# A mixed-layer inference step on one core: gate products placed one by one, states written out in two halves, expert weights loaded earlier, and 72 instead of 48 weight chunks on eleven places

## The reference, cut to what matters

```
P  = rmsnorm(x) @ w_in                      # 1024 x 5888, split among heads and two gates
x  = x + (sigmoid(G_a) * (HGRN2(P) @ w_branch_a) + sigmoid(G_b) * (RWKV7(P) @ w_branch_b)) @ w_out
x  = x + moe(rmsnorm(x))                    # 32 experts, top 4 per token
y  = rmsnorm(x)

def expert_block(tok, e):                   # every expert runs
    h = x[tok] @ w_gu[e] + b_gu[e]          # 1024 x 2048
    act = glu * sigmoid(1.702 * glu) * (lin + 1.0)
    return act @ w_down[e] + b_down[e]      # 1024 x 1024
```

## Time and profile before

| | us |
|---|---|
| median of three runs | 1326.92 (1326.70 to 1327.52) |
| the profiled execution, its own time | 1327.32 |
| its span, first to last instruction | 1325.6 |
| PE busy | 1288.1 (97%) |
| DVE, ACT, POOL busy | 373.8, 242.4, 52.6 |

### The profile page before, as it was taken

One profiled execution on the slowest core, in us unless ns is written; L12 is line 12 of the kernel. 1 busy time (PEld: TensorE's weight loads), 2 busy tenths in 40 slices (PEclk: granted clock), 3 DMA queues, 4 the chain that ended last, 5 costly groups with the idle time before them and its releaser, 6 DMA issues.

```text
span 1325.6 us, 18387 instructions
## 1 busy us (share of the span) xinstructions
PE 1288.1 (97%) x7355; PEld 615.1 (46%) x7355; DVE 373.8 (28%) x1019; ACT 242.4 (18%) x532; POOL 52.6 (4%) x127
## 2 busy tenths in 40 slices
PE   8999999999999999999999999999999999999997
PEld 6778768888754333333333333333333333233333
DVE  3234666554327212121121211212112111211112
ACT  3143343222122101111111111111111101111102
POOL 5000200000050000000000000000000000000000
PEclk9999899999999999999999999999999999999999
DMA  7635426110779999999999999999999999999996
GB/s 232 173 97 190 129 64 198 62 37 33 281 290 375 411 430 427 429 429 428 424 412 429 429 429 430 430 430 430 430 429 430 429 429 430 431 428 429 429 429 278
DMA packets 72720, 449.40 MB, mean 339 GB/s; under 512 B 14388, under 2 KB 43110, under 8 KB 47864
## 3 DMA queue, kind: packets, MB, share of 16 engines
q1 hardware_dynamic: 67090, 445.72, 82.2%
q10 hardware_dynamic: 5574, 2.88, 0.8%
HBM read 443.82 MB, written 4.76 MB: 338 GB/s over the span
## 4 chain that ended last, share of the span: by engine, by line
PE 75%; DMA 18%; DVE 4%; ACT 2%; issue 1%; ACTq 0%; SPq 0%; DVEq 0%
PE bank L1254 24%; PE bank L1274 13%; PE bank L553 8%; DMA ring<-in_expert_w_gu_dram 7%; PE bank L1162 5%; DMA arena<-in_expert_w_gu_dram 5%; PE bank L1193 4%; PE bank L657 3%; DMA extra<-in_expert_w_down_dram 3%; PE bank L1064 2%; DMA extra<-in_expert_w_gu_dram 2%; PE bank L1038 2%; PE bank L931 2%; ACT arena L1400 1%; PE bank L1169 1%; PE bank L914 1%
## 5 line engine op out<-in xcount | busy, mean ns | idle before, releaser
L1254 PE MATMUL bank<-arena 128*64 128x512 f32 x960 | 216.6, 594 | 1.0 <-DMA arena<-in_expert_w_gu_dram 1.0
L1400 ACT ACTIVATE arena<-bank 128x512 f32<-128x512 f32 (+6 forms) x232 | 115.5, 516 | 494.3 <-PE bank L1274 195.9
L1254 PE MATMUL bank<-ring,arena 128*64 128x512 f32 x848 | 189.6, 594 | 3.5 <-DMA ring<-in_expert_w_gu_dram 3.5
L1400 ACT ACTIVATE arena<-arena 128x256 f32<-128x256 f32 (+7 forms) x124 | 69.0, 565 | 470.9 <-DVE arena L2339 463.8
L2339 DVE TENSOR_SCALAR arena<-bank 128x256 f32<-128x256 f32 x64 | 27.0, 422 | 379.2 <-PE bank L1254 379.2
L1254 PEld LDWEIGHTS bank<-arena 128*64 128x64 f32 x960 | 67.2, 137 | 134.5 <-issue 116.9
L553 PE MATMUL bank<-arena,ring 128*128 128x288 f32 (+1 forms) x464 | 118.8, 417 | 0.5 <-ACT arena L1400 0.5
L1254 PEld LDWEIGHTS bank<-ring,arena 128*64 128x64 f32 x848 | 59.7, 137 | 115.4 <-issue 100.0
L2388 DVE COPY arena<-bank 64x512 f32<-64x512 f32 x30 | 20.8, 694 | 319.6 <-PE bank L1274 319.6
L553 PEld LDWEIGHTS bank<-arena,ring 128*128 128x128 f32 x464 | 89.0, 193 | 28.5 <-issue 1.9
L1274 PE MATMUL bank<-arena 128*64 128x512 f32 x448 | 100.6, 595 | 0.0
(11 more groups left out here) (371 smaller groups left out, 1130.7 us busy)
## 6 DMA issues: line engine op xcount, KB each, us to landing
arena<-in_expert_w_gu_dram SPq DMA_DIRECT2D x60, 2048.0 KB, 23.5
ring<-in_expert_w_gu_dram SPq DMA_DIRECT2D x53, 2048.0 KB, 20.6
ring<-in_expert_w_down_dram SPq DMA_DIRECT2D x28, 2048.0 KB, 20.5
arena<-in_expert_w_down_dram SPq DMA_DIRECT2D x28, 2048.0 KB, 26.8
extra<-in_expert_w_gu_dram SPq DMA_DIRECT2D x15, 2048.0 KB, 22.5
ring<-in_w_in_dram SPq DMA_DIRECT2D x23, 1024.0 KB, 5.4
extra<-in_expert_w_down_dram SPq DMA_DIRECT2D x7, 2048.0 KB, 31.7
ring<-in_w_out_dram SPq DMA_DIRECT2D x4, 1024.0 KB, 7.0
```

The source lines that it names most:

```text
L1254: ins = mm(bank[q % 2][64 * (q // 2):64 * (q // 2) + 64, :], gu_lhs(c), w[:, q * 512:(q + 1) * 512], start=(c == 0), stop=(c == KT - 1), s ...
L1400: return nc.scalar.activation(out, in_, f, **kw)
```

## The change

- Gate products are no longer placed by tiles in the front but by single products: 3, 3, 2, 5, 1, 1, 1, 8 in the samples' RWKV stage, then 1, 1, 1, 2, 1, 9, 6, 3 and the rest up to 56 in the HGRN2 stage. In the units the four products of site Y move to A5, which then has five; the sum of a unit stays 18.
- The HGRN2 states of the samples go out in two transfers of 1 MB, after `hg_upd` 4 and 8. DVE waits for the first before its masks, ACT for the second before the first squares.
- The last two w_out chunks are loaded when the HGRN2 stage has ended; chunk 3 is issued right behind chunk 2, chunks 0 and 4 before the wait for `merged` 8, chunk 5 behind it.
- 72 chunks instead of 48 use eleven places (`HEAD_QUADS` = 3): three quads are written out, and the eight places come after.
- For the first pair POOL makes `ind`, and PE no longer waits for `gsel_ready` before the first expert's bias; the wait stands before `gt_T`.
- PE runs seven spare products, five before the first transposes and two before the first projection.

```diff
-WS, FULL = 8, 11
+WS, FULL, HEAD_QUADS = 8, 11, 3
-        PEELED = 2 * QUAD * ECH
+        PEELED = HEAD_QUADS * QUAD * ECH
-        btmp = PQ[:, 0:NT]
+        btmp = fm[9][:, 0:NT]
-        FILL = (("Y1", 1), ("A0", 1), ("A1", 1), ("A3", 1), ("A4", 1), ("A5", 1), ("Y", 4), ("k0", 0), ("k1", 0), ("k2", 0), ("k3", 1),
+        FILL = (("Y1", 1), ("A0", 1), ("A1", 1), ("A3", 1), ("A4", 1), ("A5", 5), ("Y", 0), ("k0", 0), ("k1", 0), ("k2", 0), ("k3", 1),
                 ("c0", 2), ("c1", 1), ("c2", 1), ("c3", 3))
...
-            for n in list(range(N_IN + 4)) + [N_IN + 6, N_IN + 7, N_IN + 4, N_IN + 5]:
+            for n in list(range(EARLY)) + [N_IN + 6, N_IN + 7] + list(range(EARLY, N_IN + 6)):
                 if n == N_IN + 6:
-                    sp.wait_ge(S("oa_done"), 9)
+                    sp.wait_ge(S("hg_state"), 8)
+                    sp.wait_ge(S("hg_o_evac"), 3)
                     sp.wait_ge(S("rws_out"), 16 * NB)
                 if n == N_IN + 4:
                     sp.wait_ge(S("rwp_out"), 16)
                     w_load(sp, 0, 2)
+                    w_load(sp, 0, 3)
...
+            w_load(sp, 0, 0)
+            w_load(sp, 0, 4)
             sp.wait_ge(S("merged"), 8)
-            w_load(sp, 0, 0)
             for x in (0, 2, 3):
                 sp.dma_start(braw[NE * x:NE * x + NE, :], expert_b_gu[0]).then_inc(S("braw_loaded"), 16)
-            for s in (3, 5):
-                w_load(sp, 0, s)
-            sp.wait_ge(S("wo_done"), 1)
-            w_load(sp, 0, 4)
+            w_load(sp, 0, 5)
...
+            keep_busy(5, bank[5])
             for t, (o, n) in enumerate(TILES):
                 pe.wait_ge(S("xn_done"), t + 1)
...
+            keep_busy(2, bank[5])
             pe.wait_ge(S("xT_evac"), 5)
...
+            def gate_run(to):
+                while gate_m[0] < to:
...
+            def gate(n):
+                gate_run(gate_m[0] + n)
...
-                gate_tile()
+                gate(3)
                 for G in range(2):
+                    if G:
+                        gate(3)
                     for b in range(NB):
...
-                gate_tile()
+                gate(5)
                 for j in range(3):
+                    if j:
+                        gate(1)
...
                 if t:
-                    gate_tile()
+                    gate(3)
                 pe.wait_ge(S("hg_kT_evac"), i3 + 1)
                 if t:
                     pe.wait_ge(S("hg_upd"), 8)
...
                 if t:
-                    gate_tile()
+                    gate_run(KT * WHOLE)
                 for c in range(4):
...
+                    if t == 0:
+                        gate(1)
                     pe.wait_ge(S("hg_state"), g)
...
                 for g in range(2):
-                    gate_tile()
+                    gate((9, 6)[g])
...
             pe.wait_ge(S("hg_state"), 8)
-            pe.wait_ge(S("rw_in"), 1)
...
-            pe.wait_ge(S("bgu3"), 1)
+            pe.wait_ge(S("bgu3"), 2)
...
                     if c == 6:
-                        if x == 0:
+                        if x == 0 and not first:
                             pe.wait_ge(S("gsel_ready"), i + 1)
...
                     if x == 1:
+                        pe.wait_ge(S("gsel_ready"), i + 1)
                         gt_T()
...
+            def sample_states_out(g):
+                act.wait_ge(S("hg_upd"), 4 * g + 4)
+                b = slice(4 * g, 4 * g + 4)
+                act.dma_start(hgrn_s[0, b].rearrange("b h k v -> k (b h) v"),
+                              s0h.rearrange("p (b h v) -> p b h v", b=NB, h=HA)[:, b].rearrange("p b h v -> p (b h) v"))\
+                   .then_inc(S(f"hgrn_out{g}"), 16)
...
+                    sample_states_out(0)
                     keys_evac(2, 1)
-                    act.wait_ge(S("hg_upd"), 8)
-                    act.dma_start(hgrn_s[0].rearrange("b h k v -> k (b h) v"), s0h.rearrange("p (b h v) -> p (b h) v", b=NB, h=HA))\
-                       .then_inc(S("hgrn_out"), 16)
+                    sample_states_out(1)
...
+                if u == 0:
+                    act.wait_ge(S("hgrn_out1"), 16)
                 square_evac(0)
...
-                    dve.wait_ge(S("hgrn_out"), 16)
+                    dve.wait_ge(S("hgrn_out0"), 16)
...
+            for x in range(2):
+                step(g.tensor_scalar(ind[:, x * SLOTS:(x + 1) * SLOTS], bcast(pmod, [P, SLOTS]), float(x), None, ALU.is_equal), "bgu3")
```

More of the change, by code:

```diff
@@ L312, in pe_place @@
         def pe_place(quad, s):
-            return place((quad if isinstance(quad, int) else 2) * (QUAD * ECH) + s)
+            return place((quad if isinstance(quad, int) else HEAD_QUADS) * (QUAD * ECH) + s)
         def pe_w_wait(quad, s):
@@ L323, in pe_w_wait @@
                 per_quad = QUAD * ECH // WS
-                nc.tensor.wait_ge(w_loaded[place(n)], quad * (16 * per_quad) + 16 * (loads_into(place(n), n + 1) - 2 * per_quad))
+                nc.tensor.wait_ge(w_loaded[place(n)], quad * (16 * per_quad) + 16 * (loads_into(place(n), n + 1) - HEAD_QUADS * per_quad))
         def acc(t):
@@ L475, in expert @@
                 return sp.value_load(bt[0:1, bass.ds(quad * QUAD + j, 1)], min_val=0, max_val=NE - 1)
-            with sp.Fori(3, last) as quad:
+            with sp.Fori(HEAD_QUADS + 1, last) as quad:
                 for j in range(QUAD):
@@ L534, in _, with keep_busy @@
             done(i, "par_T")
+            def keep_busy(n, b=bank[1]):
+                for _ in range(n):
+                    mm(b[:, 0:P], ident, ones, start=True, stop=True)
+            keep_busy(5, bank[5])
             for t, (o, n) in enumerate(TILES):
@@ L628, in _ @@
                 done(i, "smp_pe")
[L630 to L649, removed]
+            gate_m = [0]
+            def gate_run(to):
+                while gate_m[0] < to:
                     g, kt = gate_m[0] // KT, gate_m[0] % KT
@@ L660, in fill @@
                         done(i, "pj_done")
+            def gate(n):
+                gate_run(gate_m[0] + n)
+            def fill(u, site):
+                gate_run(gate_products(u, site))
             vR, At, Rt, Bn, Kn = fm[2], fm[5], fm[6], fm[7], fm[8]
@@ L743, in smp_states @@
                     done(i, "smp_pe")
-                gate_tile()
+                gate(8)
                 for q in range(4):
@@ L751, in _ @@
             smp_scores()
+            gate(2)
             smp_solve()
@@ L1100, in last_logits @@
                 return i
-            def keep_busy(n, b=bank[1]):
-                for _ in range(n):
-                    mm(b[:, 0:P], ident, ones, start=True, stop=True)
             w_out_tile(2, acc(2))
@@ L1364, in pe_last @@
                     done(ins, "wo_done")
-            for quad in range(2):
+            for quad in range(HEAD_QUADS):
                 for p in range(2):
@@ L1370, in _ @@
             last = pe.value_load(nblk[0:1, 1:2], min_val=0, max_val=(BLOCKS - NE) // QUAD) + (NE // QUAD - 1)
-            with pe.Fori(2, last) as quad:
+            with pe.Fori(HEAD_QUADS, last) as quad:
                 for p in range(2):
@@ L2366, in gather_rows @@
                 for x in range(2):
-                    v.tensor_scalar(ind[:, x * SLOTS:(x + 1) * SLOTS], ones[:, 0:SLOTS],
-                                    gselc[:, x * TW + 6:x * TW + 7], None, ALU.mult)
+                    if not (isinstance(i, int) and i == 0):
+                        v.tensor_scalar(ind[:, x * SLOTS:(x + 1) * SLOTS], ones[:, 0:SLOTS],
+                                        gselc[:, x * TW + 6:x * TW + 7], None, ALU.mult)
                     ins = onehot(gsel, x * SLOTS, P, gselc[:, x * TW:x * TW + 3], gselc[:, x * TW + 3:x * TW + 6])
@@ L2524, in _ @@
                 step(g.tensor_tensor(braw[r, :], braw[r, :], bgu3[r, :], ALU.subtract))
-                i = g.tensor_copy(bgu3[r, :], braw[r, :])
-                step(i, "bgu3" if r.start == 96 else "pool_step")
+                step(g.tensor_copy(bgu3[r, :], braw[r, :]))
+            for x in range(2):
+                step(g.tensor_scalar(ind[:, x * SLOTS:(x + 1) * SLOTS], bcast(pmod, [P, SLOTS]), float(x), None, ALU.is_equal), "bgu3")
             pool.wait_ge(S("logits"), 2)
```

12 lines of the change are left out of this document (6 added, 6 removed).

## The result

The changed kernel takes 1320.17 us (median of five runs, 1319.95 to 1320.58) against 1327.52 (1326.70 to 1327.93) of the kernel before on the same chip: a ratio of 0.9944, 95% interval [0.9931, 0.9956], 7.35 us less. The prediction was 1317.4, inside its range of 1313.0 to 1322.0, and 2.8 us too low: 2.15 because the gain was to be 9.5 us and is 7.35, 0.6 because the kernel before takes 1327.52 us here and not the 1326.92 from which the forecast was counted. The profiled execution took 1319.95 us, its span is 1318.2.

The account below looks back on a forecast made before the run. The prediction took the weight stream from chunk 6's issue to bound the kernel: -4.2 and -2.2 us until chunk 6, then -1.4 and -1.7 for holes, -9.5 in all, giving 1317.4 us, range 1313.0 to 1322.0.

Parts of the forecast that it names:

- What bounds the kernel: Whole kernel: the weight stream sets the end, counting from chunk 6's issue, which the front's PE work decides.
- The check of the sum: Weight stream: chunk 6's issue at 399.8, 185 chunks, two holes and slow start give 1306 to 1309, against 1306.9.
- Gate products before R: Front, before the units: single products keep the clock at 1.00 and fill idle PE time; -4.2 us (bounds -1.0 and -5.9).
- the clock falls all the same: Rival, front near 156 us: the clock still halves despite the split, so 2.4 us is missing, 1319.8; chance 0.20.
- Spare products: Front, before first transposes and projection: seven products' cost stands against an earlier clock rise; 0 (bounds +0.5 and -0.8).
- States in halves: Front, before unit 0's masks: both 1 MB transfers, 6 us each, land in time; zero, letting the 4.2 us through.
- Five ahead of R: In each of four units: Y's products moved ahead fill PE's 0.56 us wait for DVE; -2.2 us (bounds 0 and -2.4).
- Early loads: Front: loading chunks 0, 3, 4, 5 sooner gains nothing, as chunk 6 still waits for PE, and w_out has room; zero.
- The hole at chunk 15: Stream at 440 to 445 us: without PE's wait before the first bias, chunk 15 is issued in time; -1.4 us (bounds 0 and -1.4).
- The hole at chunk 56: Stream near 663 us: with 72 chunks on eleven places the wait moves to chunk 80 and vanishes; -1.7 us (bounds 0 and -1.8).

Follow-up runs that it names:

- e5: The changed kernel with the 56 gate products before the units in whole tiles of eight again, at the seven sites of before; 1325.21 us.
- e10: The changed kernel with the samples' HGRN2 states going out in one 2 MB transfer after the last update, awaited by DVE before the first masks; 1322.49 us.
- e8: The changed kernel without the seven spare products; 1320.64 us.
- e6: The changed kernel with only the first eight gate products (3, 3, 2 around the 64x8 products) in one whole tile again; 1323.25 us.
- e7: The changed kernel with one product at A5 and four at Y in each unit, as before; 1322.13 us.
- e3: The changed kernel with `ind` made by DVE again and PE waiting for `gsel_ready` before the first bias; 1320.57 us.
- e1: The changed kernel with two quads written out again, so 48 chunks on eleven places; 1319.55 us.
- e2: The kernel before the change, with only 72 chunks on eleven places (three quads written out) added; 1329.35 us, ratio 1.0005.
- e11: The changed kernel with chunk 6 issued right behind the last product using its place, and two w_out row pairs moved ahead of the third tile's transposes; 1323.79 us.
- e4: The changed kernel with a hole made on purpose: chunk 94 is issued only when chunk 93 has landed; 1323.51 us.
- e12: The changed kernel with chunk 6 issued sooner, two w_out row pairs moved ahead of transposes, and 48 chunks on eleven places; 1321.04 us.

## Why the prediction was right, and where it was off

- **What bounds the kernel**: right. In e5 to e10 chunk 6 is issued 393.3 to 396.1 and the stream's time stays within 906.1 to 906.9; what the front gains or loses is the gain or loss. The check of the sum agreed by luck: it counts 185 chunks up to the landing at 1306.9, but that is the last landing but one, the 184th. The 4.9 us too many stood for a start slower than the 2 us allowed (the first two chunks land at 413.96, 14.1 us after the issue of chunk 6 and not 9.8) and for losses such as the 1.3 us at 621.98, beside the instruction load at 617.6. The forecast used only differences, in which this cancels.
- **Gate products before R, -4.2**: unit 0 starts 5.25 us sooner. The places of the gate products are worth 3.05 of it (e5, where the half clock lasts 3.4 us). The half clock of the kernel before lasted 6.8 us, which adds some 1.7 by an estimate (half of the 3.4 us more), and about 0.5 are left, for which e8 shows no sure cause. The clock stayed up, by the split around the 64x8 products (e6): the rival "the clock falls all the same" (0.20) is out. It is the largest part of the gain.
- **Spare products, 0**: at most -0.5 to -0.7 (e8), inside the bounds, and not shown to be theirs.
- **States in halves, 0, lets it through**: right; with one transfer chunk 6 comes 1.7 us later (e10). The halves took longer than the 6 us each: issued at 193.75 and 197.87, they landed at 201.17 and 208.75, 7.4 and 10.9 us later, still ahead of the first mask (207.75) and of ACT's first square (211.20).
- **Five ahead of R, -2.2**: the mechanism was right, the size was not: -1.5, by the profiles of before and after and by removal (e7). The sum let the products fill the whole 0.56 us before R. The idle time of the piece from A5 to the chunk products fell from 0.56 + 0.17 + 0.39 to 0.38 + 0.17 us, and the five products' weights load in 2.24 us, against 0.30 + 1.75: 0.57 - 0.19 = 0.4 us a unit, not 0.55.
- **Early loads, 0**: not tried by themselves. Nothing waits for w_out's chunks, and what is left between the start of unit 0 and chunk 6 is explained by the units.
- **The hole at chunk 15, -1.4**: the mechanism was right (no wait, chunk 15 issued sooner, 436 GB/s), the early part of the stream is 1.2 us shorter (e3 has 1.1), but by e3 only 0.4 (median) to 0.8 us (landing) of it are left at the end.
- **The hole at chunk 56, -1.7**: this is the step that failed: "Chunk 56 is the first that waits ... (429 - 357)/429 x 10 = 1.7 us". The hole closed, and no other opened, but a hole counts for what the slowest DMA engine loses, and in the later stream this engine still had work when the others stood still. In the kernel before the first landing at this hole came 2.4 us late (7.32 us after the one before), the last one 0.1 (5.00), and the landings moved from 3.3 to 1.0 us apart; the chunk behind them lost 0.9 (5.75), beside the instruction load at 671.07. Between the chunks that land near 471 and near 766 the changed kernel needs 294.92 us, the kernel before 295.27: 0.35 us for the closed hole, net of what instruction loads cost in both. The four instruction loads of the third written-out quad then cost 1.1 us (439.37 in e1, 440.46 in the changed kernel), by the one at 819.46 alone. The prediction left them out. e1 and e2 show the sum of both from either side: 72 chunks for 48 cost between 0 (the stream in e2) and 0.6 us (the median in e1).
- Terms as measured: 6.75 (5.25 up to unit 0, 1.5 behind it) + 0.6 for both holes less the instruction loads = 7.4 us.

Which engine an instruction load delays, and whether the loads could be spread so that none becomes the last, stays open: the trace doesn't name the engine.

## What to carry to other kernels

When a stream of large transfers sets the end, don't price a hole by the bytes that are missing: read the 16 landings of a transfer, and count what the last engine loses. A small hole can cost the last engine nothing and still draw the engines together, so that the next instruction load counts in full. Writing out a loop to get better buffers costs instruction loads: here four more, each of which set one DMA engine back by 1.5 to 1.7 us. Products placed as filling can do more than fill idle time: the tile split around the 64x8 products kept the clock up (e6), and taking products out of the waits of PE was followed in e11 by its fall.

An edit that moves chunk 6 by a few tenths is compared stage by stage, not by the total: unit 0 started up to 0.7 us apart in kernels that don't differ ahead of it (206.37 in e3, 207.04 in e7).

## What was not expected of the hardware

The landings of the 16 DMA engines drift apart: from 2.1 us at 471 us to 6.0 at the end of the changed kernel, and stay closer together (2.4 us) behind a hole in which the first ones wait (e4). From the last landing of one chunk to that of the next, issued just then, the slowest engine loses 2.9 us (e4).

The clock fell in two ways. At 156 us it falls with PE busy 2.00 of 2.00 us behind 64x8 products, and three larger products between and two behind prevent it (e6); it doesn't fall without the spare products either (e8). In e11 it fell at 400 us, for 10.2 us, behind a stretch in which PE was idle 1.0 of 5.0 us, 0.69 us the longest at a time; e12 has the same stretch without the fall in its profile, and runs that lie 4 us apart. The Trainium skill ("TensorE: Matmul & The Clock Gate", HAM oscillation) asks to avoid idle gaps, and speaks of long ones. At 156 us none precedes the fall, and those of e11 are short and didn't bring the clock down in e12: the rule explains neither fall.
